# A two-block transformer kernel: raw rows are transposed right after the experts, and the norms' row factor goes onto the results

## The reference, cut to what matters

```
x = x + hier_moe(rms_norm(x, ffn_norm), ...)     # top 2 of 64 experts
x = rms_norm(x, final_norm)                      # end of the first block
xn = rmsnorm(x, pre_mix_norm)                    # second block, token_mixer
proj = xn @ w_in                                 # rq, rk, rv, rg, cq, ckv, kr
rq, rk = rope(rq), rope(rk)
ret_out = silu(rg) * head_groupnorm(retention(rq, rk, rv))
```

## Time and profile before

| what | value |
|---|---|
| runs shown | 2042.19 us median of 3 (2040.62 to 2044.79) |
| profiled execution, first to last instruction | 2036.1 us; no time of its own is given beside the span |
| PE busy | 1766.1 us, 87% |
| DVE busy | 902.1 us, 44% |
| ACT busy | 738.8 us, 36% |
| POOL busy | 265.5 us, 13% |
| granted TensorE clock, mean | 0.963 of 2.4 GHz |

### The profile page before, as it was taken

The page is one execution under the profiler, slowest core; times in us unless marked ns, Lnnn a source line. Parts: engine busy times, 40 slices in busy tenths (PEclk is TensorE's granted clock), DMA queues, the critical chain, the costliest instruction groups (busy, mean ns, idle before and its releaser), DMA issues.

```text
span 2036.1 us, 37869 instructions
## 1 busy us (share of the span) xinstructions
PE 1766.1 (87%) x15190; PEld 1275.6 (63%) x15190; DVE 902.1 (44%) x1699; ACT 738.8 (36%) x1382; POOL 265.5 (13%) x281
## 2 busy tenths in 40 slices
PE   7999999787877777787778777779989999999998
PEld 5677788644444444444444444458867799998877
DVE  5555335532222222232222223266265698886245
ACT  4444522233222322222232222252365554445143
POOL 0000000000000000000000000640010078880000
PEclk9999999899998998998999889999999999999999
DMA  6222222799999999999999999944230233333322
GB/s 209 79 84 69 78 102 91 309 371 421 427 425 427 426 426 427 426 426 426 427 425 427 426 427 426 421 144 113 79 95 1 73 94 115 108 109 117 102 83 83
DMA packets 109058, 506.17 MB, mean 249 GB/s; under 512 B 9480, under 2 KB 59016, under 8 KB 75696
## 3 DMA queue, kind: packets, MB, share of 16 engines
q1 hardware_dynamic: 100864, 492.07, 60.6%
q10 hardware_dynamic: 6512, 8.94, 1.7%
q0 software_dynamic: 1600, 4.02, 0.8%
HBM read 497.32 MB, written 2.11 MB: 245 GB/s over the span
## 4 chain that ended last, share of the span: by engine, by line
PE 59%; DMA 29%; DVE 6%; ACT 2%; issue 2%; SPq 1%; POOL 0%; ACTq 0%; DVEq 0%
DMA ring<-in_w 28%; PE bank L686 13%; PE bank L687 12%; PE bank L688 12%; PE bank L2572 8%; PE bank L2484 4%; PE bank L2563 3%; PE bank L874 2%; PE bank L900 1%; PE bank L886 1%; DVE w_lo L791 1%; SPq L2115 1%; PE bank L2581 1%; DMA raw<-in_w_in 1%; ACT w_hi L775 1%
## 5 line engine op out<-in xcount | busy, mean ns | idle before, releaser
L2572 PE MATMUL bank<-ring,XTs 128*32 128x256 f32 x4032 | 284.0, 424 | 107.9 <-DMA ring<-in_w 107.1
L2827 DVE TENSOR_TENSOR x<-x,bank 128x512 f32<-128x512 f32 x264 | 163.8, 681 | 477.1 <-PE bank L2563 476.3
L2572 PEld LDWEIGHTS bank<-ring,XTs 128*32 128x32 f32 x4032 | 154.1, 119 | 238.9 <-issue 175.8
L2581 PE MATMUL bank<-ring,aT 128*32 128x256 f32 x2048 | 123.8, 381 | 90.2 <-DVE aT L2847 90.2
L2351 ACT ACTIVATE y<-bank 32x256 f32<-32x256 f32 x256 | 95.9, 375 | 225.4 <-PE bank L2563 139.0
L686 PE MATMUL bank<-hTh,w_hi 128*128 128x512 f32 x362 | 146.4, 404 | 5.8 <-DVE hTl L838 4.4
L791 DVE TENSOR_TENSOR w_lo<-raw,w_hi 128x2048 fp32r<-128x2048 f32 (+4 forms) x47 | 96.5, 2058 | 122.0 <-ACT w_hi L775 121.8
L2484 PE MATMUL bank<-arena,oh 128*32 128x256 f32 x2048 | 145.3, 422 | 4.4 <-DVE oh L2809 1.1
L2581 PEld LDWEIGHTS bank<-ring,aT 128*32 128x32 f32 x2048 | 66.5, 109 | 128.8 <-issue 96.4
L687 PE MATMUL bank<-hTh,w_lo 128*128 128x512 f32 x362 | 142.5, 394 | 0.0
L688 PE MATMUL bank<-hTl,w_hi 128*128 128x512 f32 x362 | 142.5, 394 | 0.0
(11 more groups left out here) (467 smaller groups left out, 3691.2 us busy)
## 6 DMA issues: line engine op xcount, KB each, us to landing
ring<-in_w SPq DMA_DIRECT2D x190, 2048.0 KB, 19.5
raw<-in_w_in SPq DMA_DIRECT2D x25, 1024.0 KB, 5.5
late_raw<-in_w_gate SPq DMA_DIRECT2D x11, 1024.0 KB, 5.4
late_raw<-in_w_up SPq DMA_DIRECT2D x11, 1024.0 KB, 5.3
late_raw<-in_w_down SPq DMA_DIRECT2D x11, 1024.0 KB, 5.0
raw<-in_w_out SPq DMA_DIRECT2D x4, 1024.0 KB, 5.0
third<-in_w SPq DMA_DIRECT2D x2, 2048.0 KB, 17.4
raw<-in_w_o SPq DMA_DIRECT2D x4, 1024.0 KB, 5.2
```

Source lines behind the costliest of these rows:

```text
L2572: mm = pe.matmul(Hb[BLK * j:BLK * (j + 1), :], XTs[u][:, 4 * (c % 2) + 2 * h + c // 2, :], w[:, at_:at_ + Q], start=(h == 0 and c == 0), s ...
L2581: mm = pe.matmul(Yb[BLK * j:BLK * (j + 1), :], aT[:, r, h, :], ring[3 * u + 2][:, at_:at_ + Q], start=(h == 0 and r == 0), stop=(h == 1 an ...
L2827: ins = v.tensor_tensor(xs, xs, Sb[t % 2][n][:, :], ALU.add)
```

## The change

- After the last pair PE scatters features 0 to 511 of all four tiles first, then features 512 to 1023 (`scatter_half`). DVE adds half a tile at a time.
- Right behind, PE transposes the raw x (`turned_half`), banks 0 to 3 while the second half is being scattered, banks 4 to 7 after the last flush. Nothing is scaled before; xn4 is gone.
- The splits into hTh and hTl come at once. Squares, means and roots follow behind them, for four tiles together, and so does the low half of rq's second unit. The early Sqrt on ACT is gone.
- The first unit's halves are made inside the last pair, before the last copies of y2. Of these copies ACT makes two and DVE two.
- The row factor is put onto the results. For rv and lat it is a scale of ACT's copies. For rq, rk and rg, where rows lie along the free axis, a product of ones by a diagonal spreads it over 128x512 (`rowscale`, one more bank, between rq and rk); cos2 and sin2 are multiplied by it, and rg before its silu, by DVE.
- The banks from rk on are one further than before.

```diff
-        plan("hT3", DC)
+        J["hT3"] = [bk.take(1, (c,))[0] for c in range(DC)]
+        bk.next = 0
         plan("rq", RH, "each")
+        plan("rowscale", 1)
...
         def pe_second(pe):
-            pe_to_feature(pe, J["hT3"], lambda i, c: xn4(i)[:, P * c:P * (c + 1)], lambda i: pe.wait_ge(S("xn4"), i + 1))
             pe_feature(pe, "rq", hT, fresh="hT3")
+            job = J["rowscale"][0]
+            claim(pe, job)
+            pe.wait_ge(S("diag"), 1)
+            fill(pe.matmul(banks[job.bank][:, :], C("ones"), diag, start=True, stop=True), job)
...
# dve_second
             v.wait_ge(S("sines"), 4)
+            read(v, J["rowscale"])
+            v.tensor_tensor(cos2, cos2, row_scale, ALU.mult)
+            chain(v.tensor_tensor(sin2, sin2, row_scale, ALU.mult))
...
+            v.wait_ge(S("x2"), NT)
+            for c, job in enumerate(J["rg"]):
+                ahead(lo_until, v, "rg", c)
+                full(v, job)
+                free(v.tensor_tensor(rgT[:, c, :], banks[job.bank][:, :], row_scale, ALU.mult), job)
             read(v, J["rv"])
...
# act_second (rv and both halves of lat get scale=rstd2[:, i:i + 1])
+            job = J["rowscale"][0]
+            full(act, job)
+            free(act.activation(row_scale, banks[job.bank][:, :], ACT.Copy), job)
             act_sines(act, "rope3", cos3, sin3)
...
             for c, job in enumerate(J["rg"]):
                 ahead(hi_until, act, "rg", c)
-                full(act, job)
-                free(act.activation(rgT[:, c, :], banks[job.bank][:, :], ACT.Silu), job)
+                read(act, [job])
+                act.activation(rgT[:, c, :], rgT[:, c, :], ACT.Silu)
...
# act_pair, after silu
+                    if u and last:
+                        hi_at.limit = len(order)
+                        hi_until(act, n_first)
                     act.wait_ge(w_used, 2 * STEPS * i + STEPS * (u + 1))
                     act.wait_ge(s_filled, 4 * i + 4)
-                    for j in range(4):
+                    for j in range(0, 4, 2 if u and last else 1):
...
             act_pair(count, True)
-            chain(act.activation(rstd2[:, 0:1], ssq[:, 0:1], ACT.Sqrt))
...
             hi_until(act, n_first + 1)
...
+            act_split_jobs(act, "hT3", hTh, lambda c: mix_gain[:, c:c + 1])
+            act.wait_ge(S("x2pre"), 1)
             for i in range(NT):
-                act.wait_ge(S("x2pre"), i + 1)
                 act.activation(xg(i), x[:, i, :], ACT.Square, accum_out=ssq[:, i:i + 1]).then_inc(S("tile_squares"), 1)
...
+            act.wait_ge(S("tile_means"), n34 + NT)
+            act.activation(rstd2, rstd2, ACT.Sqrt).then_inc(S("tile_roots"), NT)
             act_sqrt(act, "n3", rstd, NT)
...
# tensor
+            given_back(0, 4)
             for t in range(NT):
-                scatter(count + 1, t)
+                scatter_half(0, t)
+            for t in range(NT):
+                scatter_half(1, t)
+                turned_half(0, t)
+            pe.wait_ge(flushed, 4 * count + 10 + 2 * NT)
+            given_back(4, 8)
+            for t in range(NT):
+                turned_half(1, t)
             pe_second(pe)
...
# dve_pair, last
+                        lo_at.limit = len(order)
+                        lo_until(v, n_first)
+                        v.wait_ge(w_used, 2 * STEPS * i + 2 * STEPS)
+                        v.wait_ge(s_filled, 4 * i + 4)
+                        for j in (1, 3):
+                            to = 64 * (j // 2) + BLK
+                            v.tensor_copy(y2[to:to + BLK, Q * (j % 2):Q * (j % 2 + 1)],
+                                          Yb[BLK * j:BLK * (j + 1), :]).then_inc(y_out, 1)
...
+            v.sem_inc(S("x2pre"), 1)
+            dve_split_jobs(v, "hT3", hTh, hTl, lambda c: mix_gain[:, c:c + 1])
+
+            v.wait_ge(S("gain_sq"), 1)
+            for i in range(NT):
                 v.wait_ge(S("tile_squares"), n34 + i + 1)
...
+                ins = v.tensor_tensor_reduce(xg(i), xg(i), gain_sq, 1.0, 0.0, ALU.mult, ALU.add, ssq2[:, i:i + 1])
+            chain(ins)
+            chain(v.tensor_scalar(nsum, ssq, EPS / D, EPS * EPS, ALU.mult, ALU.add))
+            v.scalar_tensor_tensor(rstd2, ssq2, 1.0 / D, nsum, ALU.mult, ALU.add).then_inc(S("tile_means"), NT)
             v.tensor_scalar(rstd, ssq, 1.0 / D, EPS, ALU.mult, ALU.add).then_inc(S("norm_means"), 1)
-            lo_until(v, n_first)
+            v.wait_ge(S("tile_roots"), n34 + NT)
+            chain(v.reciprocal(rstd2, rstd2))
+            v.tensor_tensor(diag.rearrange("p (i c) -> p i c", i=NT),
...
+                            ALU.mult).then_inc(S("diag"), 1)
             v.wait_ge(S("norm_roots"), NORMS["n3"])
             v.reciprocal(rstd, rstd).then_inc(S("r3"), 1)
-            dve_split_jobs(v, "hT3", hTh, hTl, lambda c: mix_gain[:, c:c + 1])
             dve_second(v, chain, evac)
```

More of the change, by code:

```diff
@@ L1841, in act_second @@
                     act.wait_ge(S("x2"), NT)
-                free(act.activation(rv[:, i, :], banks[job.bank][:, :], ACT.Copy), job)
+                free(act.activation(rv[:, i, :], banks[job.bank][:, :], ACT.Copy, scale=rstd2[:, i:i + 1]), job)
             for c, job in enumerate(J["rg"]):
                 ahead(hi_until, act, "rg", c)
-                full(act, job)
-                free(act.activation(rgT[:, c, :], banks[job.bank][:, :], ACT.Silu), job)
+                read(act, [job])
+                act.activation(rgT[:, c, :], rgT[:, c, :], ACT.Silu)
             for i, job in enumerate(J["lat0"]):
@@ L1849, in act_second @@
                 full(act, job)
-                free(act.activation(lat[:, i, 0:LAT // 2], banks[job.bank][:, 0:LAT // 2], ACT.Copy), job)
+                free(act.activation(lat[:, i, 0:LAT // 2], banks[job.bank][:, 0:LAT // 2], ACT.Copy,
+                                    scale=rstd2[:, i:i + 1]), job)
             for i, job in enumerate(J["lat1"]):
@@ L1853, in act_second @@
                 full(act, job)
-                free(act.activation(lat[:, i, LAT // 2:LAT], banks[job.bank][:, 0:LAT // 2], ACT.Copy), job)
+                free(act.activation(lat[:, i, LAT // 2:LAT], banks[job.bank][:, 0:LAT // 2], ACT.Copy,
+                                    scale=rstd2[:, i:i + 1]), job)
             read(act, J["lat0"] + J["lat1"])
@@ L2650, in _, with given_back, scatter_half, turned_half @@
             pe.wait_ge(y_out, 8 * count + 16)
-            for t in range(NT):
-                scatter(count + 1, t)
-            pe.wait_ge(flushed, 4 * count + 14)
-            for job in J["before_moe"]:
-                pe.sem_inc(filled[job.bank], 1)
-                pe.sem_inc(freed[job.bank], 1)
+            def given_back(lo, hi):
+                for job in J["before_moe"]:
+                    if lo <= job.bank < hi:
+                        pe.sem_inc(filled[job.bank], 1)
+                        pe.sem_inc(freed[job.bank], 1)
+            def scatter_half(n, t):
+                rows_ = slice(2 * BLK * n, 2 * BLK * (n + 1))
+                pe.wait_ge(flushed, 4 * count + (10 + (t + 1 if n else 0)))
+                pe.matmul(banks[4 + t][:, :], g2[rows_, P * t:P * (t + 1)], y2[rows_, :], start=True,
+                          stop=True).then_inc(s_filled, 1)
+            def turned_half(n, t):
+                pe.wait_ge(flushed, 4 * count + (11 + NT * n + t))
+                for job in J["hT3"][4 * n:4 * n + 4]:
+                    c = job.bank
+                    if t == 0:
+                        claim(pe, job)
+                    mm = pe.transpose(banks[c][:, P * t:P * (t + 1)], x[:, t, P * c:P * (c + 1)], ident)
+                    if t == NT - 1:
+                        fill(mm, job)
+            given_back(0, 4)
+            for t in range(NT):
+                scatter_half(0, t)
[6 more added lines that the diff above has]
+                turned_half(1, t)
             pe_second(pe)
@@ L2886, in _ @@
-            lo_until(v, n_first)
+            for k in range(2 * NT):
+                n, t = k // NT, k % NT
+                v.wait_ge(s_filled, 4 * count + (5 + k))
+                v.wait_ge(flushed, 4 * count + 10)
+                xs = x[:, t, 512 * n:512 * (n + 1)]
+                v.tensor_tensor(xs, xs, banks[4 + t][:, :], ALU.add).then_inc(flushed, 1)
+            v.wait_ge(flushed, 4 * count + 10 + 2 * NT)
+            v.sem_inc(S("x2pre"), 1)
+            dve_split_jobs(v, "hT3", hTh, hTl, lambda c: mix_gain[:, c:c + 1])
@@ L2959, in _ @@
             pool.wait_ge(S("r3"), 1)
-            pool.wait_ge(S("xn4"), NT)
+            for job in J["hT3"]:
+                full(pool, job)
             for i in range(NT):
```

45 lines of the change are left out of this document (7 added, 38 removed).

## The result

The changed kernel takes 2048.41 us (8 runs, 2044.92 to 2052.54) and the kernel before, beside it, 2041.59 (8 runs). The ratio is 1.0034 (95% interval 1.0023 to 1.0045): slower, where 2039.1 with a range to 2044.8 was forecast.

The account below looks back on a forecast made before the run. PE bounds the kernel, standing still before rq. Job three of rq gains 4.4 us, less 0.45 and 0.85 is 3.1: span 2033.0 for 2036.1, plus 6.1 gives 2039.1 us, range 2034.8 to 2044.8.

Parts of the forecast that it names:

- Step 2: Last scatters to rq: half scatters at 0.43 us each with raw transposes between; rq starts at 1341.1.
- Step 4: PE's clock behind the gap grown from 1.77 to 5.7 us: a loss of 1.0 us, bounds 0 and 3.3.
- the clock stays at 1.2 GHz into rq: Rival: thin work behind the 5.7 us gap keeps PE's clock low over 16 us; slower, 2047.1 us at 18 us; 11%.
- Step 1: y2 copies behind the split of rq's first unit, plus increments: scatters start at 1332.4, 4.0 us later than before.
- Step 3: Norm chain ahead of the low half of rq's second unit: PE stalls 1.4 us at job three; Sqrt's table costs nothing.
- the third rival: Sqrt's table load lies on the path at the norms: 1.3 to 2.7 us more stall, 2040.4 to 2041.8 us; 8%.
- Step 5: Row factor's later costs: ones-by-diag product 0.45 us, bank shift at the retention's first product 0.85, nothing in lat0.

Follow-up runs that it names:

- All but halves: The version with all five orders mended, but its last scatters back to feature halves; 2.5 us worse than that version by distance to the kernel before.
- low half early: Changed kernel with rq's second low half made ahead of the norm products and Sqrt's table loaded ahead of the splits; median 9.0 us above the kernel before.
- by tiles: Changed kernel with the last scatters tile by tile on both sets of 64 rows, flushed by halves; ratio 0.9997 to the kernel before.
- unit behind, tiles: Changed kernel with rq's first unit split behind the y2 copies and the last scatters by tiles; ratio 0.9997, median 1.2 us above the kernel before.
- halves on the kernel before: Kernel before with only its last scatters and flushes by feature halves; median of 11 runs 5.4 us above the kernel before.
- all: Changed kernel with tile scatters, early increments, first unit behind y2, early low half and table, row-factor product in bank 7; median 3.6 us below the kernel before.
- the best version: The version with all five orders mended, plus DVE's first angles moved behind the low half of rk's second unit; 2034.18 us, ratio 0.9961.

## Why the prediction was wrong

Two steps failed, each mis-sized by about the same amount, and the experiments show that they act together.

**Step 2, the half scatters.** It read 0.43 us per half scatter (two instructions) from the earlier trace rows, where two half scatters ran at a time, and kept that price for a form in which mostly only one can. Shown: alone a half scatter takes 0.86 us at 2.4 GHz and 1.7 at 1.2 GHz. The forecast had 8.7 us from the scatters to rq; measured were 15.9. "All but halves", with the same form at full clock, tells the parts:

| part | forecast | at 2.4 GHz throughout | changed kernel |
|---|---|---|---|
| first scatter to first transposes | 2.2 | 3.6 | 7.0 |
| three rounds of scatter and transposes | 2.7 | 4.9 | 4.9 |
| from there to rq | 3.8 | changed by other edits | 3.9 |

So the form costs 3.6 us more than forecast even at full clock: 1.4 in the first part and 2.2 in the rounds, of which 1.3 are the half scatter at 0.86 and the rest, 0.3 a round, the change between scatters and transposes. The Trainium skill (TensorE: Matmul & The Clock Gate, Why this matters for your kernels) has the rule, with figures for groups of 32 rows: products with few rows run at once when each lies in its own group of rows, and one alone takes as long as a full one. The rows agree that they run at once: 1.13 for four instructions on both sets, 1.12 for two on one set.

**Step 4, the clock,** was priced at 1.0 with 3.3 as its bound. The table shows 3.4 in the first part alone, and 1.6 more were lost behind the stall at job three. The clock falls in the gap: in every profile here with a gap of 2.29 us or more ahead of the last scatters it was low before they began or within 0.4 us after, and in none with 1.77 or less. How long it stays low goes with the form of the work: 3.4 to 6.8 us with tiles, 10.2 to 23.9 with halves. Two pairs of profiles differ in little else: with a gap of 6.83, 6.8 with tiles and 23.9 with halves ("low half early"); with 2.3, 3.4 and 23.9. As an estimate (half of the time at half clock) 23.9 us cost up to 12. So the rival "the clock stays at 1.2 GHz into rq" was real in three of the profiles (it reached rq's first products), though not in that of the changed kernel, where the clock was back at +12.8. That thin work (products of 64 rows with short transposes between) keeps it down alone is not shown: "all but halves" kept 2.4 GHz through all of its halves behind a gap of 1.41. What all the profiles fit is that it takes both, a gap in which it falls and thin work behind it. Nor does the length of a gap decide alone: at job three waits of 2.3 ("by tiles") and 2.9 ("unit behind, tiles") left the clock at 2.4 GHz, and in the norms' gap of "halves on the kernel before" it fell 1.2 us after PE's last scatter.

**Step 1, y2,** was right: ready 4.76 us behind the down product for a forecast 5.35, and the scatters at +5.96 for +5.75. The total agrees by luck, as two errors cancel. DVE's copies take 0.44 each (0.4 priced), the landing came 0.8 sooner, but eight increments take 1.2 where 0.3 were priced. The bound of 1.3 for all 16 was too low as well: they take 2.4 to 2.6. The nearest row, an increment between ACT's root and DVE's reciprocal, was of other engines and could not bound PE's.

**Step 3, the stall,** was 2.29 for 1.4. The price of nothing for Sqrt's table was wrong. The load began 0.08 us after DVE's last mean, at 1363.53, and took 1.28 us on the path. The Silu row has its load ahead of the wait, which its ACTIVATE carries; here the wait is a record of its own (1363.484) and the load stands behind it. So the third rival's mechanism holds, at 1.3. Of the drain of 1.38 us that the Trainium skill (ScalarE: Activation LUTs, What ACT_TABLE_LOAD costs) adds, the rows show nothing: the root follows at 1364.82, directly behind the load.

**Step 5** was right in most: 0.9 for the bank shift (0.85 priced), no wait in lat0, 0.69 for each of cos and sin. The ones-by-diag product costs 0.9, twice its price of 0.45, in the changed kernel as in "by tiles" and "all". Rk's low half behind the angles was a trap: no wait for it in the changed kernel, 1.2 us in "low half early" and 2.6 in "all".

The prediction's own sums hold but for 0.1 to 0.2: its terms put rq at 1341.0 (it has 1341.1) and diag with r3 at 1351.4 (1351.2), and the 7.1 us in lat0 leave out the 0.2 by which rg's last product starts later. None of this changes the outcome.

The sum put job three at +27.9; it came at +35.4. Of these 7.5 us, 7.4 are rq's late start, 0.9 the stall and 0.2 the pace of the first two jobs, less the 1.0 set aside for the clock. Transposing raw rows and putting the factor on later does give time: with the costs above mended the kernel is 6.1 us below the one before.

**What stays open.** In the traces the best version is 8.8 us shorter than the kernel before, counted behind the down product, and 6.1 in the medians; "halves on the kernel before" is 0.7 longer in its trace and 5.4 in the median; "by tiles" is 3.1 shorter than the changed kernel in its trace and 7.2 in the median. A profile shows one execution, and executions of one kernel differ by 5 to 15 us. That of the kernel before is a short one: with the 1.8 us that lie between span and time in the changed kernel's, it took 2037.9 (an estimate), below all eight runs beside the changed kernel. The clock is the likely reason, since a run's time falls with its mean granted clock (correlations of -0.58 to -0.91 in each of the twelve kernels here with more than one run, the changed one among them), but what it did in the seam of the unprofiled runs was not seen. The end of the down product lies at 1326.3 to 1332.9 in the profiles of the changed kernel and its variants and at 1326.7 to 1329.9 in those of the kernel before; whether the change costs time ahead of it was not tested. Why the low clock lasted 3.4 us in one and 23.9 in another was not settled either.

## What to carry to other kernels

Before a matmul is cut in halves, see which rows it uses and whether its price was read beside a partner on the other rows; cut so that both sets stay in the queue. A gap on PE ahead of thin work can cost more than its length, so keep it short (here 1.8 us ahead of the scatters left the clock up, while 2.3 did not), and count what seems free towards it, such as bare increments. When two costs are coupled by the clock, mending one alone may show nothing: undo each from the version that has all of them.

## What was not expected of the hardware

- Products on rows 0–63 and 64–127 ran side by side even when the queue held two of one set first (1.99 us for eight in either order). A product of the other set started up to 1.1 us ahead of products queued before it (+3.37 and +4.49), yet its increment landed in the queue's order (+5.13 behind +5.09).
- A bare semaphore increment in PE's queue takes 0.15 to 0.16 us (eight in a row 0.15 apart; 16 lengthen a gap by 2.57).
- Behind a gap of only 2.29 us the granted clock was 0.51 for 23.4 us in which PE was 95% busy:

```profile
1329.60:1353.00 23.40, 22.18 (x53) 11.60 (x54) 11.88 (x16) 6.95 (x10) 0.00 (x0) 0.51 0.20 59
```
